# A two-block transformer kernel: Strassen weight granules split four places ahead, the first group's products reordered

## What is computed

```python
def rmsnorm(x, g):
    xf = x.astype(jnp.float32)
    y = xf * lax.rsqrt(jnp.mean(xf * xf, axis=-1, keepdims=True) + EPS)
    return (y * g.astype(jnp.float32)).astype(x.dtype)

def swiglu(x, w_gate, w_up, w_down):           # 1024 -> 2 x 2816 -> 1024
    return (jax.nn.silu(x @ w_gate) * (x @ w_up)) @ w_down

x = x + 0.5 * swiglu(rmsnorm(x, ffn1_norm[l]), ffn1_w_gate[l], ffn1_w_up[l], ffn1_w_down[l])
...
return rmsnorm(x, final_norm)
```

## Time and profile before

| | |
|---|---|
| median of 3 runs | 1359.53 us |
| the profiled execution | 1361.13 us, its span 1359.3 us |
| TensorE busy (weight loads beside it) | 1326.7 us, 98% (82%) |
| VectorE, ScalarE, GpSimd busy | 68%, 60%, 36% |
| mean granted TensorE clock | 0.991 |
| costliest VectorE line | L375, `wlo`, 189 times, mean 2.35 us |
| chained transfers (GpSimd, 1 MB) | 32, median 9.3 us from issue to landing |
| plain up loads (SP, 1 MB) | 85, median 5.4 us |

### The profile page before, as it was taken

One profiled execution on the slowest core, in us unless ns is written; L12 is line 12 of the kernel. 1 busy time (PEld: TensorE's weight loads), 2 busy tenths in 40 slices (PEclk: granted clock), 3 DMA queues, 4 the chain that ended last, 5 costly groups with the idle time before them and its releaser, 6 DMA issues.

```text
span 1359.3 us, 18294 instructions
## 1 busy us (share of the span) xinstructions
PE 1326.7 (98%) x7252; PEld 1113.8 (82%) x7252; DVE 930.1 (68%) x1162; ACT 814.2 (60%) x1095; POOL 493.7 (36%) x220
## 2 busy tenths in 40 slices
PE   9998999999999999999999999999999999999897
PEld 8887777888887888887888887788888888888786
DVE  6778886955577896687886559754335632567887
ACT  7646467456654557655567787667434654654663
POOL 1623213473641504532314231035525524462320
PEclk9999999999999999998999999999999999999999
DMA  9587884234568796577784645355854544648783
GB/s 342 187 211 249 236 288 154 97 97 164 204 163 232 217 266 227 185 183 253 203 289 155 229 175 194 121 182 177 290 183 155 198 143 148 208 156 212 242 211 109
DMA packets 42279, 269.66 MB, mean 198 GB/s; under 512 B 6321, under 2 KB 6865, under 8 KB 11217
## 3 DMA queue, kind: packets, MB, share of 16 engines
q1 hardware_dynamic: 35680, 226.69, 47.5%
q0 software_dynamic: 4608, 33.56, 13.1%
q10 hardware_dynamic: 1904, 8.23, 1.7%
HBM read 267.38 MB, written 1.08 MB: 197 GB/s over the span
## 4 chain that ended last, share of the span: by engine, by line
PE 47%; DVE 4%; POOL 4%; issue 3%; DMA 1%; ACT 1%; POOLq 0%; DVEq 0%; ACTq 0%
PE acc L394 9%; PE acc L396 9%; PE acc L395 9%; PE acc L409 6%; PE acc L410 3%; POOL forms L1010 2%; DVE wlo L375 2%; PE acc L2821 2%; DMA raw<-in_t_ffn_down 1%; POOL forms L1017 1%; PE acc L2822 1%; PE work L657 1%; PE work L658 1%; PE work L659 1%; PE work L1172 1%
## 5 line engine op out<-in xcount | busy, mean ns | idle before, releaser
L375 DVE TENSOR_TENSOR wlo<-raw,whi 128x2048 fp32r<-128x2048 f32 (+1 forms) x189 | 443.4, 2349 | 125.4 <-ACT whi L370 125.0
L370 ACT ACTIVATE whi<-raw 128x2048 fp32r<-128x2048 f32 (+1 forms) x245 | 459.8, 1886 | 102.1 <-DMA raw<-in_t_ffn_down 74.9
L409 PE MATMUL acc<-xT,whi 128*128 128x512 f32 x1208 | 429.9, 398 | 4.2 <-DVE wlo L375 3.6
L375 POOL TENSOR_TENSOR wlo<-raw,whi 128x2048 fp32r<-128x2048 f32 x56 | 271.7, 4853 | 347.8 <-ACT whi L370 339.9
L410 PE MATMUL acc<-xT,wlo 128*128 128x256 f32 x1384 | 374.0, 281 | 0.0
L409 PEld LDWEIGHTS acc<-xT,whi 128*128 128x128 f32 x1208 | 226.9, 188 | 61.2 <-issue 7.8
L410 PEld LDWEIGHTS acc<-xT,wlo 128*128 128x128 f32 x1384 | 261.4, 189 | 6.7
L394 PE MATMUL acc<-whi,xT 128*128 128x512 f32 x416 | 168.3, 405 | 0.0
L396 PE MATMUL acc<-whi,xT 128*128 128x512 f32 x416 | 162.5, 391 | 0.0
L395 PE MATMUL acc<-wlo,xT 128*128 128x512 f32 x416 | 162.3, 390 | 0.0
L769 ACT ACTIVATE hid_hi<-work 128x256 fp32r<-128x256 f32 x88 | 33.7, 383 | 134.7 <-DVE work L867 134.7
(11 more groups left out here) (422 smaller groups left out, 2122.1 us busy)
## 6 DMA issues: line engine op xcount, KB each, us to landing
raw<-in_t_ffn_up SPq DMA_DIRECT2D x85, 1024.0 KB, 5.4
raw<-in_t_m_in SPq DMA_DIRECT2D x52, 1024.0 KB, 5.2
raw<-in_t_ffn_down SPq DMA_DIRECT2D x32, 1024.0 KB, 5.6
raw<-in_t_ffn_down POOLq DMA_DIRECT2D x32, 1024.0 KB, 9.3
raw<-in_t_m_os SPq DMA_DIRECT2D x8, 1024.0 KB, 4.8
raw<-in_t_ffn_down SPq DMA_DIRECT2D x8, 512.0 KB, 7.2
raw<-in_t_m_out SPq DMA_DIRECT2D x4, 1024.0 KB, 5.2
sum_rows<-row_scratch ACTq DMA_DIRECT2D x4, 1024.0 KB, 5.1
```

The costliest lines, as they stand in the source:

```text
L370: act.activation(granule(whi, u, i), granule(raw, u, i), ACT.Copy).then_inc(hi_ready, 1)
L375: eng.tensor_tensor(granule(wlo, u, i), granule(raw, u, i), granule(whi, u, i).bitcast(F32), ALU.subtract).then_inc(lo_signal(g)[0], 1)
L409: pe.matmul(to, hi[:, c], both_parts(kt), start=first, stop=False)
```

## The change

- `PRODUCTS` becomes one order for each group. Group 0 runs P4, P2, P3, P6, P1, P7, P5 at places 11, 13, ... 23; group 1 is as it was. P3 (place 15) now waits for the forms too. SP loads P2's weights for place 13 and P6's for 17.
- ScalarE rounds the forms of group 0 after step 10 instead of 9. VectorE makes `form_lo` at the end of steps 12 and 25 instead of at the beginning of steps 10 and 25.
- VectorE splits the granule of a product place past 13 four places ahead: in step n for place n + 4, after the additions of a product step or after `rest_hidden` of an up step. Other granules stay three places ahead.
- GpSimd issues the chained transfers for places 15 and 19 first, then `sum_hidden(1, 0)`, then those for 21 and 23.
- In FFN 3 the final norm's front half is done in step 37 instead of after the last addition.

```diff
-PRODUCTS = ("P4", "P6", "P3", "P7", "P1", "P2", "P5")
+PRODUCTS = (("P4", "P2", "P3", "P6", "P1", "P7", "P5"), ("P4", "P6", "P3", "P7", "P1", "P2", "P5"))
...
-                if name == "P6":
+                if name in ("P6", "P3"):
                     pe.wait_ge(forms_split, 2 * (2 * f + group + 1))
...
-            if n == 9:
+            if n == 10:
                 round_forms(0)
...
+        def is_early_product(n):
+            return n > 13 and n in LATE and LATE[n][0] == "product"
+
+        def lo_of_rows(n):
+            if n <= PLACES and not is_early_product(n):
+                lo(n)
+
+        def lo_of_product(n):
+            if is_early_product(n):
+                lo(n)
+
         for n in range(5, PLACES):
             entry = LATE.get(n, ("up", n))
-            if n in (10, 25):
-                rest_forms((10, 25).index(n))
...
                 join(m)
                 row(m)
-                lo(n + 3)
+                lo_of_rows(n + 3)
                 product(m)
                 rest_hidden(m)
+                lo_of_product(n + 4)
+                if n in (12, 25):
+                    rest_forms((12, 25).index(n))
             elif entry[0] == "product":
-                if n < 38:
-                    lo(n + 3)
+                lo_of_rows(n + 3)
                 add_product(n, *entry[1:])
-            elif n < 37:
-                lo(n + 3)
-            elif n == 37:
-                lo(n + 3)
+                lo_of_product(n + 4)
+            else:
+                lo_of_rows(n + 3)
+                lo_of_product(n + 4)
+            if n == 37:
+                if f == 3:
+                    finish_front(dve)
...
         add_to_slot(15)
-        add_to_slot(17)
+        add_to_slot(19)
         sum_hidden(1, 0)
-        add_to_slot(19)
+        add_to_slot(21)
         add_to_slot(23)
...
+    def finish_front(dve):
+        dve.wait_ge(final_rows_loaded, 32)
+        dve.wait_ge(resid_done, 2 * B_OUT - 1)
+        for t in range(NT):
+            dlink(dve.tensor_tensor(out_tile[:, t, FRONT], x[:, t, FRONT], gfinal2_row[:, FRONT], ALU.mult))
+        dve.wait_ge(sq_done, 2 * B_OUT + 1)
+        dlink(dve.tensor_scalar(ms[:, :], ss[:, :, 0], 1.0 / D, EPS, ALU.mult, ALU.add))
+        dwait(dve)
+        dve.sem_inc(S["out_steps"], 1)
```

More of the change, by code:

```diff
@@ L74, in late_places @@
 def late_places():
-    products = [("product", group, name) for group in range(2) for name in PRODUCTS]
+    products = [("product", group, name) for group in range(2) for name in PRODUCTS[group]]
     places = [("up", 10)]
-    for k in range(len(PRODUCTS)):
+    for k in range(7):
         places += [products[k], ("up", 11 + k)]
@@ L637, in product_index @@
     def product_index(group, name):
-        return len(PRODUCTS) * group + PRODUCTS.index(name)
+        return 7 * group + PRODUCTS[group].index(name)
     def product_bank(group, name):
@@ L643, in products_so_far @@
     def products_so_far(f, group, name):
-        return 2 * len(PRODUCTS) * f + product_index(group, name) + 1
+        return 14 * f + product_index(group, name) + 1
     BACK_OF_X = pair(0)
@@ L3171, in scaled @@
                               ALU.mult).then_inc(S["out_steps"], 1)
[L3173 to L3180, removed]
         residual_out(0)
```

## The result

The changed kernel takes 1364.39 us (median of 20 runs, 1362.12 to 1367.33) against 1359.57 us before (20 runs, 1356.77 to 1366.29): ratio 1.0032, 95% interval 1.0022 to 1.0041. It is slower by 4.8 us where 4.1 us less were forecast, and the time lies above the range. Within 0.5% of no change, as the likeliest case had it, it is.

What follows compares the result with a forecast made beforehand. TensorE was taken as held up by VectorE's late `wlo`, chiefly before P1 at place 19. Terms -21.3 - 1.5 + 14.4 + 7.2 - 2.0 - 0.95 = -4.15 us gave 1355.4 us, range 1352.7 to 1358.5.

Steps and rivals of the forecast that it cites:

- the likeliest case: Whole kernel: a measured time within about 0.5% (6.8 us) of no change, given a chance of 0.64.
- The transfer of place 19: Before P1 at place 19: issuing it ahead of the token sum removes large waits and slow products, minus 21.3 us.
- The final norm's front: End of the kernel: two multiplications and the mean square move into VectorE's idle time, minus 0.95 us.
- The new wait at P3: Place 15: TensorE waits for forms behind the chained transfer, 3.0 us in three FFNs, 4.7 in the first; plus 14.4 us.
- the load beside it: Place 17's weight load during place 15's chained transfer: landing 9.4 us after issue instead of 8.5.
- Each FFN pays about 1.8 us of one or the other: Either a slower clock after P3 or a wait before P6 at place 28, in each FFN: plus 7.2 us.
- The early splits taken as free: VectorE's pair of places: 8.54 us against TensorE's 8.37, the 0.17 excess carried by the split-ahead margin.
- Small old waits: Small waits behind P1, 4 us left in the old kernel: half credited as gone, minus 2.0 us.
- (a): Place 15's transfer undisturbed by load 17, no clock fall: P3 waits 2.0 us (3.8 first FFN); 1351.8 us, chance 0.20.
- (c): Waits behind the forms don't bind because VectorE is ahead, so all gains stay: 1334 us, chance 0.06.
- (b): Load 17 delays place 15's transfer by its full 2.5 us and the clock falls everywhere: 1361.4 us, chance 0.14.
- (d): VectorE's pair of places becomes the bound at 8.9 us, TensorE losing 0.53 a pair: 1370.4 us, chance 0.08.

Runs made afterwards that it cites:

- e2: Kernel before, with only GpSimd's chained transfer of place 19 issued ahead of the token sum of group 1: 1336.00 us, ratio 0.9833.
- e7: Changed kernel with all splits three places ahead again, everything else as changed: 1354.13 us, ratio 0.9971 to before.
- e5: Kernel before, with place 19's transfer ahead of the token sum and the final norm's front half in step 37: 1334.73 us, ratio 0.9829.
- e3: Changed kernel, but SP issues the load of place 17 only after the chained transfer of place 15 has landed: 1360.49 us, ratio 1.0007 to before.
- e6: e2 plus splits of products past place 13 made four places ahead; forms and product order as before: 1354.28 us, ratio 0.9965.
- e9: e2, but in up steps from place 12 the split stands behind product and rest, still three places ahead, uncovering the silu: 1376.28 us, ratio 1.0119.
- e12: e6, with a product step's additions moved between row and product of the following up step, covering the silu: 1348.90 us, ratio 0.9922.
- e13: Changed kernel, with a product step's additions moved between row and product of the next up step: 1363.17 us, ratio 1.0035 to before.

## Why the forecast was wrong

**Right.** The transfer of place 19: the wait at P1 and its slow product go and half of the small waits with them, 22.9 us measured by e2 (24.8 in the stretches) against 23.3 in the forecast. The final norm's front: 0.9 in the profile, 0.95 forecast. The new wait at P3, its releaser, VectorE's stand for the chained transfer and the load beside it (about 1.0 against 0.9): 15.7 us of waits against 14.4. Nearly every sign that the forecast named came out, and the time was wrong all the same, since each sign allowed more than the sum had in it.

**Wrong, by term.** The sum for the four stretches was -3.2 us and they gave +4.1, so 7.3 are missing.

- *"Each FFN pays about 1.8 us of one or the other"* (the clock after P3 or the wait at P6): plus 7.2. Both came in three FFNs. The clock fell at P3 in all four, 7.0 us, and P6 waited 3.1 us besides. The step assumed that TensorE made later by the slow product gives VectorE time. It does, but VectorE's walk from the first forms to the second was costed at 57.6 us and took 58.6 in every FFN; a split slowed beside GpSimd's sum, 3.14 us at 421.15 and not in the old order, is most of that. Short by 2.9 us. Rows of before did show falls after 3.18 us and more; the three forecast waits of 3.0 us sat just beneath, and the forecast left them open. The measured ones were 3.5 to 4.5, and the experiments show falls after less than 2.
- *P3's wait* itself: short by 1.3 us.
- *The early splits taken as free* outside group 0's forms. In the first FFN VectorE stands for the chained transfer of place 30 and at an uncovered silu: 2.9 us at places 31 and 33, not foreseen, and 1.6 more for the slow up piece at place 31. At the second FFN's end the transposes for the norm after it wait 2.4 us for `x_gained` against 0.5 before, since VectorE stands for the granule of place 38 ahead of the residual (2.00 us at 511.89). 1.5 of it lie in the stretch.
- *Small old waits*: credited with 2.0, and all 4 went. That takes 2 off again.

These are 2.9 + 1.3 + 4.5 + 1.5 - 2.0 = 8.2. The many other pieces that ran a little over their 2.73 and 5.64 us give back about 0.9 (4.5 us over before, 3.6 now), which makes the 7.3.

e7 weighs the early splits as a whole: without them the changed kernel takes 1354.1 us, near the forecast of 1355.4. Part of that is luck, since in e7 too P3, its slow products and P6 cost 23.7 us where 21.6 were forecast, and the small waits give 2.0 more. But the step that the forecast put at next to nothing, splitting the products four places ahead, is worth 8 to 10 us, more than all that is missing.

The view that misled is the order of the sum. Term by term against the old profile it looked like a trade in which a known 21 us was paid for 21.6. Against e5, which has the two good edits alone, the other edits cost 29.7 us by the medians (27.6 by the ratios, 29.4 in the stretches), and little was left for them to win: in e2 TensorE waits 3.3 us in all for `wlo`.

**The rivals.** (a) and (c) are out by P3's wait. (b) is out in its cause by e3, but the clock did fall at all four P3s as it had it, and its 1361.4 us is the rivals' time nearest to the measured one. (d), VectorE's pair as the bound, was given 0.08 because the excess of 0.17 us a pair seemed small beside the margin. The mechanism, an early order that costs VectorE its lead, is real: 18 us on top of the good order. In the changed kernel the early splits cost 8 to 10, but mostly in the first FFN and not pair by pair: in FFNs 1 to 3 it is 3.7 us, 1.5 of them the wait for `x_gained`. The error in its weighing was to compare 8.54 with 8.37 and not with 8.00: what is lost is also the 0.37 us a pair by which VectorE used to catch up after the forms.

**Open.** The 18 us of e6 are placed (group 0, and group 1 of the first FFN), but the shares of silu, slowed splits and standing for transfers were separated only by sums of rows: e9, e12 and e13 each changed more than one of them, and no kernel kept GpSimd's sums away from the splits. The late forms and the new order of group 0 were measured only together. Why the clock falls after 1.82 us of waiting and stays after 3.42 isn't settled.

## What to carry to other kernels

Cost each edit against the kernel that has the other edits, not only against the old one; where one edit removes the bound, the rest may be pure cost. A step that looks idle between two dependent instructions may be the cover of another engine's work: before it is moved, ask what was computed under it, and what else will lie there. An engine that is slightly faster than the bound pays back its debts at the difference; half a microsecond a round can take the whole difference away without making it the bound by the averages.

## Hardware seen on the way

GpSimd's sum and VectorE's split exclude each other. In e2 the sum starts 0.17 us behind a split, takes 4.40 us, and the split keeps its 2.28; the next split starts at 408.52, as the sum ends (408.51):

```profile
403.94 2.28 DVE L375 TENSOR_TENSOR wlo<-raw,whi 128x2048 fp32r<-128x2048 f32 x1
...
404.11 4.40 POOL L1017 TENSOR_TENSOR forms<-hid_hi,hid_lo 128x1024 f32<-128x1024 f32 x1
```

In e6 the sum (412.50 to 416.87) is delayed by one split and then delays the next, which starts at 415.85 and takes 3.17 us: 416.87 and a split's 2.2 is 419.0. In e12 the next split follows at once and pays the most, 2.2 us. Who comes second pays. The Trainium skill's page "SBUF — State Buffer" says so under "Summary: rules for kernel authors": with two SBUF inputs on VectorE the second to issue blocks until the first is done. These rows agree.
